# Six modulation sums ahead of the attention steps and four behind them, with the attention's weights asked for two sums sooner

## What is computed

```python
ml = (jax.nn.silu(c) @ mod_w[i] + mod_b[i])[:, None, :]      # mod_w: (2, 1024, 6144)
sh1, sc1, g1, sh2, sc2, g2 = jnp.split(ml, 6, axis=-1)
hl = xl * (1.0 + sc1) + sh1
...
yl = diff_attention(ql, concat([kl, kc]), concat([vl, vc]), lam, subln, wo, lam_init)
xl = deepnorm_update(xl, yl, g1, ln_g[i, 0], ln_b[i, 0])
tokens = (xl * (1.0 + sc2) + sh2).reshape(B * S, D)
y2 = moe_ffn(tokens, router_w, router_b, moe_wg[i], moe_wu[i], moe_wd[i])
xl = deepnorm_update(xl, y2, g2, ln_g[i, 1], ln_b[i, 1])
```

## Time and profile before

| | us |
|---|---|
| median of 3 runs | 1201.13 (1200.76 to 1202.65) |
| the profiled execution | 1202.47 |
| its span, first to last instruction | 1200.6 |
| PE busy in the span | 1133.3 (94%) |
| DVE busy | 362.8 (30%) |
| ACT busy | 166.8 (14%) |
| moved by DMA | 480.17 MB, mean 400 GB/s |

### The profile page before, as it was taken

The page is one execution under the profiler, slowest core; times in us unless marked ns, Lnnn a source line. Parts: engine busy times, 40 slices in busy tenths (PEclk is TensorE's granted clock), DMA queues, the critical chain, the costliest instruction groups (busy, mean ns, idle before and its releaser), DMA issues.

```text
span 1200.6 us, 12399 instructions
## 1 busy us (share of the span) xinstructions
PE 1133.3 (94%) x5282; PEld 493.3 (41%) x5282; DVE 362.8 (30%) x733; ACT 166.8 (14%) x397; POOL 8.0 (1%) x10
## 2 busy tenths in 40 slices
PE   8997998899999999999998889999999999988986
PEld 3543554545444333343333227543333433333322
DVE  1569899663111111111111115212111111111113
ACT  1201233514100000001000005200000100000000
POOL 0000000000000000000000010000000000000000
PEclk9998999899999999999999999999999999999999
DMA  9999897983999999999999999999999999999994
GB/s 387 407 376 379 289 361 269 400 321 158 431 429 430 433 429 430 430 431 430 431 430 430 431 424 430 424 429 432 431 429 432 430 430 433 430 430 430 431 430 182
DMA packets 41017, 480.17 MB, mean 400 GB/s; under 512 B 5120, under 2 KB 6400, under 8 KB 9472
## 3 DMA queue, kind: packets, MB, share of 16 engines
q1 hardware_dynamic: 39904, 476.91, 94.7%
q10 hardware_dynamic: 1056, 2.43, 0.7%
HBM read 476.18 MB, written 1.05 MB: 397 GB/s over the span
## 4 chain that ended last, share of the span: by engine, by line
PE 74%; DMA 18%; DVE 6%; ACT 1%; issue 1%; another core or an unknown queue 0%; SPq 0%; DVEq 0%
PE ps L910 44%; DMA ring<-in_moe_wu 16%; PE ps L902 5%; PE ps L918 4%; PE ps L664 3%; DMA ring<-in_mod_w 2%; PE ps L759 2%; PE ps L667 2%; DVE ring L1342 1%; PE ps L722 1%; PE ps L607 1%; PE ps L670 1%; PE ps L740 1%; DVE modp L1342 1%; PE ps L928 1%; PE ps L582 1%
## 5 line engine op out<-in xcount | busy, mean ns | idle before, releaser
L910 PE MATMUL ps<-ring,tra 128*64 128x512 f32 x2048 | 453.9, 597 | 24.2 <-DMA ring<-in_moe_wu 19.3
L910 PEld LDWEIGHTS ps<-ring,tra 128*64 128x64 f32 x2048 | 147.6, 138 | 322.3 <-issue 281.1
L910 PE MATMUL ps<-ring,work 128*64 128x512 f32 x1024 | 226.8, 595 | 1.9 <-DVE work L1693 1.9
L910 PEld LDWEIGHTS ps<-ring,work 128*64 128x64 f32 x1024 | 71.6, 137 | 135.6 <-issue 133.3
L1237 ACT ACTIVATE work<-ps 128x512 f32<-128x512 f32 x32 | 19.1, 597 | 506.5 <-PE ps L910 506.5
L1691 DVE TENSOR_TENSOR work<-work,ps 128x512 f32<-128x512 f32 x32 | 22.0, 687 | 205.7 <-PE ps L910 205.7
L1230 ACT ACTIVATE tra<-ps,cols 128x128 f32<-128x128 f32 x128 | 48.1, 456 | 255.3 <-PE ps L902 255.3
L1688 DVE TENSOR_TENSOR work<-ps,work 128x512 f32<-128x512 f32 x32 | 22.1, 691 | 202.1 <-ACT work L1237 202.1
L902 PEld LDWEIGHTS ps<-extra,xn 128*128 128x128 f32 x512 | 61.0, 195 | 24.3 <-issue 22.7
L902 PE MATMUL ps<-extra,xn 128*128 128x128 f32 x512 | 66.9, 285 | 1.4 <-DVE extra L1601 1.4
L918 PE MATMUL ps<-work,extra 64*128 64x512 f32 x256 | 63.6, 615 | 1.6 <-DVE work L1697 1.6
(11 more groups left out here) (192 smaller groups left out, 729.2 us busy)
## 6 DMA issues: line engine op xcount, KB each, us to landing
ring<-in_moe_wg SPq DMA_DIRECT2D x64, 2048.0 KB, 29.6
ring<-in_moe_wu SPq DMA_DIRECT2D x63, 2048.0 KB, 29.7
ring<-in_moe_wd SPq DMA_DIRECT2D x63, 2048.0 KB, 30.0
ring<-in_mod_w SPq DMA_DIRECT2D x40, 1024.0 KB, 9.6
ring<-in_mod_w SPq DMA_DIRECT2D x4, 2048.0 KB, 17.1
ring<-in_attn_wqkv SPq DMA_DIRECT2D x4, 2048.0 KB, 11.4
ring<-in_attn_wo SPq DMA_DIRECT2D x2, 2048.0 KB, 11.2
ring<-in_tokens SPq DMA_DIRECT2D x4, 512.0 KB, 18.0
```

The source lines that it names most:

```text
L910: last = mm(ps[SLOTS * h:SLOTS * h + SLOTS, b, :], lhs(k0 + k), w[:, k, h * NB:(h + 1) * NB], start=(k0 + k == 0), stop=(k0 + k == KT - 1) ...
```

## The change

It alters four things, and computes the same:

- DVE does six sums (0 to 5) ahead of the steps, with both rope batches ahead of the sixth; ten in the steps (now 6 to 15); then sum 16 behind `norm_heads(0)`, 17 and 18 behind `norm_heads(1)`, and 19 inside `attention_norm`, between the two halves of the tokens.
- PE's row batches stand behind groups 8, 13, 17 and in step 11 (before: 6, 10, 15 and 19), and the fifth behind the last projection. DVE's sum of layer 1's rows moves into `route`, PE's wait for it to the gather ahead of the first expert. As bank 7 holds rows for longer, the turned latents use bank 0 instead.
- SP asks for `("q", 1)` ahead of sum 7 (before: ahead of 9), for `("v", 1)` ahead of 11 (before 13), for `("wo", 0)` ahead of 14 (before 15), for the input x and `("wo", 1)` ahead of 16 (before 18), and for expert units 1 to 5 ahead of sum 18 and unit 6 ahead of sum 19.
- Expert unit 8 goes to slot 1 and unit 9 to slot 3 (before the other way round), with the waits that belong to them.

```diff
-FREE = (10, 4, 8, 5, 9, 6, 7, 2, 3, 1, 0)
+FREE = (10, 4, 8, 5, 9, 6, 7, 2, 1, 3, 0)
...
-BATCH_AT = {6: 0, 10: 1, 15: 2, 19: 3}
-
-EARLY_SUMS = 8
+BATCH_AT = {8: 0, 13: 1, 17: 2, 21: 3}
+
+EARLY_SUMS = 6
 STEP_SUMS = 10
+ROPES_AT = 5
...
-LOADS = [("q", 0), 0, 1, ("v", 0), 2, "rows", 3, 4, ("k", 1), 5, 6, 7, 8, ("q", 1), 9, "ahead", 10, 11, 12, ("v", 1), 13, 14,
-         ("wo", 0), 15, 16, 17, ("wo", 1), "x", 18, 19]
-AHEAD = 1
+LOADS = [("q", 0), 0, 1, ("v", 0), 2, "rows", 3, 4, ("k", 1), 5, 6, ("q", 1), 7, "ahead", 8, 9, 10, ("v", 1), 11, 12, 13,
+         ("wo", 0), 14, 15, "x", ("wo", 1), 16, 17, ("e", 1), ("e", 2), ("e", 3), ("e", 4), ("e", 5), 18, ("e", 6), 19]
+AHEAD, ISSUED = 1, 7
...
-                elif v in (7, 8):
-                    sp.wait_ge(sem("half_summed"), 2 * (NSUM - 8 + v))
-                elif v < RING:
-                    sp.wait_ge(sem("unit_used"), NA - RING + v + 1)
+                elif v in (7, 9):
+                    sp.wait_ge(sem("half_summed"), 2 * (NSUM - 1 if v == 7 else NSUM))
+                elif v in (8, 10):
+                    early_used(sp, ("wo", (v - 8) // 2))
...
             job(4)
-            row_batch(4)
-            NT_BANK = (4, 6, 5, 7)
+            NT_BANK = ((4, 6, 5, 0), (4, 6, 5, 7))
...
             project(1, 1)
-            pe.wait_ge(sem("rows_ready"), 2)
+            row_batch(4)
...
-                keep_clock(NT_BANK[2], 3)
+                keep_clock(5, 3)
                 turn_normed(layer, 1)
-                keep_clock(0, 1)
+                keep_clock(1, 1)
...
                 turn_weights().then_inc(sem("sw_turned"), 1)
+                if layer == 0:
+                    pe.wait_ge(sem("rows_ready"), 2)
                 gather(7, 1).then_inc(sem("gather_done"), 1)
...
             for n in range(EARLY_SUMS):
-                if n == 6:
-                    rope_batch(0)
+                if n == ROPES_AT:
+                    for batch in range(2):
+                        rope_batch(batch)
                 unit_sum(n)
-            rope_batch(1)
...
                 if s == NS:
                     norm_heads(0)
+            unit_sum(NSUM - 4)
             job_out(3)
             heads_variance(1)
             norm_heads(1)
-            for n in range(EARLY_SUMS + STEP_SUMS, NSUM):
-                unit_sum(n)
+            unit_sum(NSUM - 3)
+            unit_sum(NSUM - 2)
             job_out(4)
...
                     if t == 0:
-                        rows_sum(1)
+                        unit_sum(NSUM - 1)
...
                 for t in range(TT):
                     normed_out(layer, t)
+                if layer == 0:
+                    rows_sum(1)
                 dve.wait_ge(sem("logits_done"), layer + 1)
```

More of the change, by code:

```diff
@@ L509, in load_expert @@
             def load_expert(layer, e):
-                for n in range(AHEAD if layer == e == 0 else 0, EU):
-                    load_unit(layer, e, n)
+                for n in range(EU):
+                    if first_unit(layer, e) + n >= ISSUED:
+                        load_unit(layer, e, n)
             for what in LOADS:
@@ L520, in _ @@
                     load(xn[:, :].rearrange("p (t n) -> p t n", t=TT), x[0].rearrange("(t p) n -> p t n", p=P), sem("x_loaded"))
+                elif isinstance(what, tuple) and what[0] == "e":
+                    load_unit(0, what[1] // EU, what[1] % EU)
                 elif isinstance(what, tuple):
@@ L843, in turn_normed @@
                     normed(pe, 2 * layer, t, b)
-                    turn_blocks(NT_BANK[2 * t + b], xn[:, t * D + b * NB:t * D + (b + 1) * NB]).then_inc(sem("nT_done"), 1)
+                    turn_blocks(NT_BANK[layer][2 * t + b], xn[:, t * D + b * NB:t * D + (b + 1) * NB]).then_inc(sem("nT_done"), 1)
             project(1, 0)
@@ L1525, in normed_out @@
                 dve.wait_ge(sem("nT_done"), 4 * layer + 2 * t + 2)
-                v_.tensor_copy(nT[:, 4:8, t * P:t * P + P], bank((6, 7)[t]).rearrange("p (k t) -> p k t", k=4))\
+                v_.tensor_copy(nT[:, 4:8, t * P:t * P + P], bank((6, 0 if layer == 0 else 7)[t]).rearrange("p (k t) -> p k t", k=4))\
                     .then_inc(sem("nT_dve"), 1)
```

## The result

The changed kernel takes 1190.71 us (median of 4, 1190.26 to 1193.26) against 1201.42 (median of 4, 1200.76 to 1202.65) for the kernel before on the same chip: ratio 0.9914, interval 0.9897 to 0.9931. That is 10.3 us less by the ratio and 10.7 by the medians. The profiled execution is the one of 1190.69 us, with a span of 1188.8 against 1200.6: 11.8 less.

A forecast was written before the change was run, and what follows sets the result against it. The prediction took expert loads as the bound, the end following expert 0's start one for one. With 10.3 us ahead at step 12 and nothing lost behind, 1201.13 - 10.3 gave 1190.8 us; range 1187.5 to 1195.5.

The forecast's parts named there:

- The bound: Expert loads set the pace from about 300 us; the end moves one for one with expert 0's start.
- Ahead of the steps: Up to `scores(0)`: PE's three waits for DVE go and the clock stays up; PE 10.7 us ahead from step 4.
- Steps 4 to 9: DVE's work unchanged, its last step sum ending at 195.8; PE 11.8 us ahead without row batch 3.
- Steps 10 to 12: PE waits 3 us for sum 15 ahead of row batch 3; part of the gain is paid back, leaving 10.3 us.
- the three cases: Clock in steps 10 to 12: low throughout, never falling, or falling and returning; 9.4, 12.2 or 10.4 us ahead.
- the third case: Steps 10 to 12: clock falls and returns 5.8 us after PE resumes, at 201.6; 10.4 us ahead, rounded down to 10.3.
- The second case: Steps 10 to 12: clock never falls, PE's pieces end at 201.1, DVE's chain at 202.2; 12.2 us ahead.
- Behind the steps: Sums 16 to 19, the row sum and batch 4 fit into idles and cost nothing, with 0.8 us of cover where thin.
- the first rival: Behind the steps, sum 18 lands late and delays `project(1, 0)`; 1 to 5 us lost, 1191.8 to 1196; chance 0.13.
- `route`: The row sum moves into an idle of 3.78 us there at no cost; a clock dip more or less is in the range.
- The rival of a held-up queue: SP's order holds sum 18 back behind units 1 to 5, 15.7 us late: 1206.5; chance 0.03.

The follow-up runs named there:

- seven_ahead: The changed kernel with seven sums ahead of the steps and nine in them, instead of six and ten: 1188.35 us, ratio 0.9896 to the kernel before.
- the repeat: The changed kernel unaltered, compared a second time with the kernel before: 1191.06 us against 1203.86, ratio 0.9890.
- fill_heads: The changed kernel with one filler matmul ahead of the last step's first turning of probabilities and two behind it: 1190.30 us, ratio 0.9896 to the kernel before.
- sum18_first: The changed kernel with the load of sum 18 ahead of expert unit 5 in SP's queue: 1190.11 us, ratio 0.9886 to the kernel before.
- fill_and_first: The changed kernel with both the three fillers at the heads and sum 18's load ahead of unit 5: 1187.53 us, ratio 0.9865 to the kernel before.
- old_loads: The changed kernel with SP asking for the attention's weights at the sum numbers of the kernel before: 1204.67 us, ratio 1.0020 to the kernel before.
- all_edits: The changed kernel with seven sums ahead and nine in the steps, fillers at the heads, and sum 18's load ahead of unit 5: 1183.82 us, ratio 0.9851.

## Why the prediction was right

The forecast was 1190.8 and a gain of 10.3; measured were 1190.71 and a gain of 10.3 by the ratio, 10.7 by the medians, 11.8 in the profiled pair, and 12.8 to 13.2 when it was compared once more. So the time is well predicted, and the gain is right to some 3 us. Step by step, with expert 0 starting 12.0 sooner in the profiled pair:

- **The bound.** Unit 11 was to be issued near 281 and was at 279.17, with the DMA at rest before; one for one from there, as the table shows.
- **Ahead of the steps**, right: `scores(0)` 102.1 forecast, 101.40 measured, the scores and group 11 at full clock (1.13 and 7.13). Group 12 was to be 11.8 ahead and was 122.95 - 110.58 = 12.4 ahead. Half a us of that was there before the change acts: the trace after is 0.5 ahead already in group 6.
- **Steps 4 to 9**, right: the last step sum was to end at 195.8, and row batch 3, which waits for it, began at 195.11. That DVE carries this stretch agrees with seven_ahead, where one step sum less takes the wait away.
- **Steps 10 to 12**, the term that was mis-sized. Forecast was a wait of 3 us, measured 2.10. Forecast was the clock's return at 201.6, 5.8 us after PE resumes as in the kernel before; it came by 198.8, 3.7 us after. So `scores(12)` started 212.37 - 200.49 = 11.9 ahead and ended 12.8 ahead, where I took 10.3; of the three cases it lay near the second, which I hadn't taken. Part of that is an error in the third case itself: with the clock back at 201.6 the pieces from there to 203.0 are halved as well as `scores(12)`, which then ends 11.1 ahead and not 10.4. (The second case has a slip too: halved, its pieces end at 200.4 and not 201.1, which changes nothing, as it goes by DVE's chain.) The rest is the last step sum, 0.7 us earlier than forecast, and the clock. In the repeat it came back some 5.2 us after PE resumed, near the 5.8 of the forecast, and `scores(12)` ended 12.0 ahead.
- **Behind the steps**, "all that costs nothing" was wrong by 2.2 us, from 12.8 ahead to 267.21 - 256.64 = 10.6, in two places. The first took it to 235.80 - 224.50 = 11.3: the lower clock lasted from the idle ahead of 216.37 to 222.5, through more of the last products and turnings than before. fill_heads shows that fillers in PE's idle there keep the clock up, but the same idle stood in the kernel before, so why the dip was longer isn't shown; in the repeat it was shorter and nothing was lost here (235.80 - 223.72 = 12.1). The second took the other 0.7: sum 18 landed late. I had its first half wanted at 234.3 and moved by 231.8 plus landing; DVE got it at 234.76, after 1.64 us of waiting, 0.9 of it covered. That is the first rival, in part: sum18_first took the wait away, and fill_and_first showed its price. The order within SP's queue, named beside it from the Trainium skill (DMA: Bandwidth & Descriptors, Queues, rings and completion order), is in agreement with this but isn't tested by it: with its load ahead of unit 5, sum 18 no longer had unit 5's bytes before it, but it was also issued at 219.88 instead of 224.01, as SP no longer waited for the last values first.
- **`route`** gave 1.4 back, from 10.6 to 287.47 - 275.47 = 12.0: the router's products took 1.94 us at the lower clock in the profiled execution before (274.16), and 1.07 in the one after (263.04), and the filler in front of them 1.55 and 1.02. A dip more or less was in the range. The repeat had one more, of 1.6 us, ahead of expert 0, which then started 11.2 sooner.

So the forecast is right in its main terms, and that it came out as near as this is luck: an error of 2.5 us at steps 10 to 12 and one of 2.2 behind them cancel, they measured 0.8 and 1.6 us less in the repeat's trace, and the gain itself was 2 to 3 us larger in the second comparison. Sums 16 and 19 did hide, as said; the row sum did too (wait of 3.78 before, 0.96 after). The rival of a held-up queue didn't come up: unit 1 went out at 195.45 and unit 2 at 197.10. What the prediction passed over in a sentence was the loads of the attention's weights: without their earlier places the whole change is 1.6 us slower than the kernel before by the medians, 2.4 by the ratio (old_loads, 1.0020), not 10.3 faster.

## What to carry to other kernels

Find the one point after which the rest of a program is of fixed length (here the first use of the ring's first slot, with a DMA at rest before it), and read everything ahead of it as a chain: in thirteen profiled executions the end followed that point within 0.7 us. When sums or other fillers are moved between an engine's waits, check the chain of each engine on its own: a filler is free only up to the other branch's length, and shortening one of two near-equal branches pays in full only once the other is shortened too (0.7 and 0.3 us alone in the traces, 1.9 together). And before a forecast is called exact, compare the same two kernels twice: here the gain was 10.7 us once and 12.8 the other time. When work moves earlier, its loads must move with it: the wait for a late one costs its length and the clock behind it.

## What was not expected of the hardware

The lower clock's length varied between equal stretches. At steps 10 to 12 it lasted some 10 us in the kernel before (from within 204 to 206 to within 214 to 216). There the changed kernel had it for some 3.4 us in one execution (from within 194 to 196 to within 198 to 200) and for some 6.8 in the other (from within 192 to 194 to within 200 to 202), around the same wait of 2.10 us. Between the same two executions the products at the heads took 2.05 us once (216.37) and 1.49 the other time:

```profile
216.78 1.49 PE L744 MATMUL ps<-ring,tra 128*128 128x128 f32 x8 [1.76 <-ACT ring L1181]
```

Three fillers, in 2.9 us of idle, kept it at its upper level there, in the traces of all three kernels that have them (fill_heads, fill_and_first, all_edits).
